# The inverse of chunks 4 to 7 kept in the other half of the partitions, in a fused two-layer decoder kernel

## The reference

```python
def step(state, inp):
    rt, wt, kt, vt, kkt, at = inp
    sa = jnp.einsum("bhvk,bhk->bhv", state, -kkt)
    state = (state * wt[:, :, None, :] + sa[..., None] * (kkt * at)[:, :, None, :]
             + vt[..., None] * kt[:, :, None, :])
    return state, jnp.einsum("bhvk,bhk->bhv", state, rt)
...
y = rwkv7_scan(r, decay, k, v, kk, a)
```

## Time and profile before

| what | value |
| --- | --- |
| median of 3 runs | 3664.91 us |
| profiled execution | 3667.72 us |
| its span | 3665.9 us |
| TensorE busy | 3335.7 us (91%) |
| VectorE busy | 1609.7 us (44%) |
| ScalarE busy | 1316.8 us (36%) |
| mean granted TensorE clock | 0.951 |

### The profile page before, as it was taken

The page is one execution under the profiler, slowest core; times in us unless marked ns, Lnnn a source line. Parts: engine busy times, 40 slices in busy tenths (PEclk is TensorE's granted clock), DMA queues, the critical chain, the costliest instruction groups (busy, mean ns, idle before and its releaser), DMA issues.

```text
span 3665.9 us, 76910 instructions
## 1 busy us (share of the span) xinstructions
PE 3335.7 (91%) x33546; PEld 2023.8 (55%) x33546; DVE 1609.7 (44%) x3443; ACT 1316.8 (36%) x2492; POOL 223.1 (6%) x345
## 2 busy tenths in 40 slices
PE   2898998899889858999999999999999999999998
PEld 1555465456446534666656466656556656556663
DVE  7254254335434534444554244454334454334442
ACT  0343243334333334333443233443324354323332
POOL 0010001010001000000000000000000000000000
PEclk8999999999999988999989999989999999999999
DMA  7231322223133121112011211111121111121111
GB/s 322 70 94 50 111 83 82 76 70 88 70 93 108 56 93 31 43 38 67 25 43 60 76 44 60 37 37 54 42 78 42 60 38 33 58 88 38 42 50 51
DMA packets 275847, 247.30 MB, mean 67 GB/s; under 512 B 16252, under 2 KB 251960, under 8 KB 272952
## 3 DMA queue, kind: packets, MB, share of 16 engines
q1 hardware_dynamic: 273208, 233.99, 20.2%
q0 software_dynamic: 2304, 8.39, 0.6%
HBM read 217.17 MB, written 25.18 MB: 66 GB/s over the span
## 4 chain that ended last, share of the span: by engine, by line
PE 76%; DVE 11%; DMA 5%; ACT 4%; issue 2%; SPq 1%; DVEq 0%; ACTq 0%; POOL 0%; another core or an unknown queue 0%
PE bank L655 20%; PE bank L529 14%; PE bank L624 6%; PE bank L739 4%; PE bank L752 4%; PE bank L562 3%; PE bank L748 3%; PE bank L526 3%; DVE xm L1534 3%; PE bank L604 3%; DVE arena L1595 2%; PE bank L666 2%; DMA xm<-in_ada_w 2%; PE bank L794 1%; DMA arena<-residual_scratch 1%
## 5 line engine op out<-in xcount | busy, mean ns | idle before, releaser
L655 PE MATMUL bank<-xm,wring 128*128 128x512 f32 x2048 | 947.8, 609 | 0.8 <-ACT arena L1083 0.8
L655 PEld LDWEIGHTS bank<-xm,wring 128*128 128x128 f32 x2048 | 386.5, 195 | 468.8 <-issue 457.6
L529 PE MATMUL bank<-arena,wring 128*128 128x512 f32 x1280 | 580.0, 593 | 13.4 <-ACT xm L948 5.1
L529 PEld LDWEIGHTS bank<-arena,wring 128*128 128x128 f32 x1280 | 231.0, 190 | 257.5 <-issue 246.0
L624 PE MATMUL bank<-wring,yT 128*128 128x512 f32 x776 | 346.6, 609 | 23.3 <-DVE yT L1427 10.1
L624 PEld LDWEIGHTS bank<-wring,yT 128*128 128x128 f32 x776 | 150.5, 195 | 216.4 <-issue 193.1
L1129 ACT COPY arena<-bank 128x256 f32<-128x256 f32 x256 | 96.4, 377 | 452.2 <-PE bank L752 452.2
L1802 POOL COPY r_Q<-ident 128x512 f32<-128x512 f32 x160 | 98.6, 616 | 2080.5 <-PE bank L752 2078.5
L1635 DVE COPY arena<-bank 128x64 f32<-128x64 f32 x256 | 57.5, 225 | 374.5 <-PE bank L784 369.6
L752 PE MATMUL bank<-arena,r_Q 64*64 64x32 f32 x5120 | 204.3, 223 | 0.0
L739 PE MATMUL bank<-arena 64*64 64x32 f32 x5120 | 196.4, 224 | 1.7 <-DVE arena L1619 1.0
(11 more groups left out here) (276 smaller groups left out, 5136.6 us busy)
## 6 DMA issues: line engine op xcount, KB each, us to landing
wring<-in_rw_w_rkvz SPq DMA_DIRECT2D x128, 512.0 KB, 4.4
wring<-in_ev_w_in SPq DMA_DIRECT2D x96, 512.0 KB, 5.3
xm<-in_ada_w SPq DMA_DIRECT2D x16, 1536.0 KB, 11.8
wring<-in_ev_w_out SPq DMA_DIRECT2D x32, 512.0 KB, 5.2
wring<-in_rw_w_out SPq DMA_DIRECT2D x32, 512.0 KB, 6.3
layer_input<-arena SPq DMA_DIRECT2D x4, 2052.0 KB, 7.6
wring<-layer_input SPq DMA_DIRECT2D x16, 513.0 KB, 6.8
xm<-in_x POOLq DMA_DIRECT2D x16, 512.0 KB, 5.4
```

The lines of the kernel that those rows point to most:

```text
L529: mm = pe.matmul(pj[:, :], w[:, k, :], hT[:, k, 1:1 + TB], start=(k == 0), stop=(k == KC - 1))
L655: mm = pe.matmul(bank[1 if m == PROJ_Z else 0][:, :], w[:, k, :], xmv[MIX_OF[m]][:, k, :], start=(k == 0), stop=(k == KC - 1))
```

## The change

The function tile gives for each chunk and head the half p (1 - h, where G and X are) and the half q, where Y and Q are; for chunks 0 to 3 q is p, for chunks 4 to 7 it is the other half. Start products of level 0 stay in p; from level 1 on they read p and write q. Columns products read q and write p, and transposed ones stay in q. Start products of all 8 chunks are one part now, and so are the columns products; in these parts chunk c and chunk c + 4 alternate. Transposed products stay in two parts. A level is start, transposed of group 0, transposed of group 1, columns. That makes 20 parts, and QUARTER_INV is new. The columns products wait for the transposed ones of their level. Y of chunks 4 to 7 is started by an extra product by the identity at level 1 and a predicated copy of its result, and no longer by VectorE's copies ahead of the first chunk. In chunks 4 to 7 the right-hand side and r_xs lie in the other half too, so that L771 and L784 stay in one half there, and L794 changes halves.

```diff
-QUARTER_INV = [[2, 1, 2, 1, 2, 0], [2, 1, 2, 1, 2, 0], [2, 1, 1, 1, 2, 0], [2, 1, 1, 1, 2, 0]]
+QUARTER_INV = [[1, 0, 1, 0, 2, 1], [1, 0, 2, 1, 0, 1], [2, 1, 0, 1, 0, 2], [1, 0, 1, 0, 1, 1]]
...
+    return (1 + (n - 1) // 4, (n - 1) % 4) if n else (0, 0)
...
+                def tile(c, h):
+                    return half_of(1 - h), half_of(h if c >= 4 else 1 - h), slice(c * 64, c * 64 + 64), c % 4 * 32
+
+                def start_of(c, h, k):
+                    p, q, cc, at = tile(c, h)
+                    return pe.matmul(packed(IV[c // 4][q if k else p, at:at + 32], 1 << k), G[p, gs_at(c, h):gs_at(c, h) + 64],
+                                     first(X[p, cc] if k else ident64[p, :], 1 << k), start=True, stop=True)
+
+                def columns(c, h, k):
+                    p, q, cc, at = tile(c, h)
+                    return pe.matmul(packed(IV[c // 4][p, 128 + at:160 + at], 1 << k), Y[q, cc], first(r_Q[q, k % 2, cc], 1 << k),
+                                     start=True, stop=True)
+
+                def transposes(c, h, k):
+                    p, q, cc, at = tile(c, h)
+                    return pe.matmul(packed(IV[c // 4][q, 256 + at:288 + at], 1 << k), r_Q[q, k % 2, cc], second(Y[q, cc], 1 << k),
+                                     start=True, stop=True)
...
+                        for c in range(4):
+                            for h in range(2):
+                                mm = start_of(c, h, k)
+                                if c == 3:
+                                    mm.then_inc(S["iq_ready"], 1)
+                            for h in range(2):
+                                mm = start_of(c + 4, h, k)
+                                if c == 3 and k != 1:
+                                    mm.then_inc(S["iqo_ready"], 1)
+                            if k == 1:
+                                for h in range(2):
+                                    p, q, cc, at = tile(c + 4, h)
+                                    mm = pe.matmul(IV[1][q, 256 + at:288 + at], ident64[p, :],
+                                                   second(G[p, gs_at(c + 4, h):gs_at(c + 4, h) + 64], 1), start=True, stop=True)
+                                    if c == 3:
+                                        mm.then_inc(S["iqo_ready"], 1)
...
+                        pe.wait_ge(S["iq"], v * 12 + 2 * k + g + 1)
                         if k == 1:
-                            pe.wait_ge(S["y0"], v + 1)
...
+                            for h in range(2):
+                                mm = transposes(c, h, k)
+                                if c == 4 * g + 3 and (g or k == LV_INV):
+                                    mm.then_inc(S["ixy_ready"], 1)
...
+                        for c in range(4):
+                            for h in range(2):
+                                mm = columns(c, h, k)
+                                if c == 3:
+                                    mm.then_inc(S["ixy_ready"], 1)
+                            for h in range(2):
+                                mm = columns(c + 4, h, k)
+                                if c == 3:
+                                    mm.then_inc(S["ixo_ready"], 1)
...
-                        pe.matmul(XB[half_of(1 - h), 0:64], G[r, g:g + 64], r_VT[r, c * RC:(c + 1) * RC], start=True, stop=False)
+                        pe.matmul(XB[at(c, h), 0:64], G[r, g:g + 64], r_VT[r, c * RC:(c + 1) * RC], start=True, stop=False)
...
+                    mm = pe.matmul(XB[at(c, h), 0:64], AR[r, c * P:c * P + 64], M[r, :], start=False, stop=True)
...
-                    mm = pe.matmul(XB[s, 64:128], Y[s, cc], r_xs[s, :], start=True, stop=True)
+                    mm = pe.matmul(XB[s, 64:128], Y[at(c, h), cc], r_xs[at(c, h), :], start=True, stop=True)
...
-                    y = Y[s, :].rearrange("p (a c x z) -> p a c x z", a=2, c=4, z=2)[:, :, :, :, 1]
-                    n = G[s, :].rearrange("p (a h c x z) -> p a h c x z", a=2, h=2, c=4, z=2)[:, :, h, :, 0:32, 1]
-                    for a in range(2):
-                        own(V.copy_predicated(y[:, a], umask[s, None, :].to_broadcast([64, 4, 32]), n[:, a]))
+                    y = Y[s, 0:256].rearrange("p (c x z) -> p c x z", c=4, z=2)[:, :, :, 1]
+                    n = G[s, :].rearrange("p (a h c x z) -> p a h c x z", a=2, h=2, c=4, z=2)[:, 0, h, :, 0:32, 1]
+                    own(V.copy_predicated(y, umask[s, None, :].to_broadcast([64, 4, 32]), n))
...
+                    V.wait_ge(S["iqo_ready"] if g else S["iq_ready"], 2 * (v * (LV_INV + 1) + k + 1))
...
+                    if k == 1 and g:
+                        V.copy_predicated(second(r_Y[v % 2][:, 256:512], 1).rearrange("p (c a) m -> p c (a m)", c=4),
+                                          umask[:, None, :].to_broadcast([P, 4, 32]),
+                                          IV[1][:, 256:384].rearrange("p (c x) -> p c x", c=4)).then_inc(S["y0"], 1)
```

More of the change, by code:

```diff
@@ L734, in invert @@
                         elif k == 1:
-                            pe.wait_ge(S["iq"], v * 12 + g + 1)
+                            pe.wait_ge(S["iq"], v * 12 + 2)
                         else:
-                            pe.wait_ge(S["ixy"], v * 10 + 2 * (k - 2) + g + 1)
-                        for c, h, r, cc, at in each:
-                            mm = pe.matmul(packed(IV[g][r, at:at + 32], m), G[r, gs_at(c, h):gs_at(c, h) + 64],
-                                           first(r_X[r, cc] if k else ident64[r, :], m), start=True, stop=True)
@@ L741, in invert @@
[L741 to L754 removed]
+                            pe.wait_ge(S["ixy"], v * 10 + 2 * (k - 2) + 2)
@@ L1629, in ahead @@
                     if v + 1 < NU:
[L1630 removed]
+                        rwkv_inverse(v + 1, COPY_CUT[3 * c + gap])
                 M = Mall[:, v % RP, :]
```

79 lines of the change are left out of this document (39 added, 40 removed).

## The result

The changed kernel takes 3679.69 us (median of 12 runs, 3675.74 to 3687.89) against 3668.8 for the kernel before timed beside it: ratio 1.0031, 95% interval 1.0022 to 1.0040, so slower by 8 to 15 us. The forecast of 3662 had the wrong sign: I had summed -3, the measurement says +11. That 3679.69 lies inside the stated range, 3637 to 3692, is owed to the width of that range and not to the sum.

A forecast was written before the change was run, and what follows sets the result against it. It took three TensorE-VectorE round trips per chunk, with floors of 0.66, 0.64 and 0.72 us, to bound the kernel. Units -4 and the first inverse +1 gave -3 us, so 3662 us, range 3637 to 3692.

The forecast's parts named there:

- Together -0.12 us per unit: Sum over an ordinary unit's four quarters, -0.18, -0.29, +0.72 and -0.37 us; over 31 units -4 us.
- my price: Inverse in each unit: an alternated part of 16 products costs 0.47 us, like a part of 8.
- The first inverse [...] +1: Inverse without chunks between its parts: waits for second copies 2.8 us, less 0.75 of (a) and some array time.
- (a): Unit start: VectorE makes two Y copies of 0.464 us instead of four; chunk 0's first gap -0.62 us.
- the fifth rival: Empty gaps pull the clock down, +11 us a unit, some +250 for most units; chance 0.02.
- Idle time over 0.2 us at the start of a level: Changed profile's inverse: TensorE idling this long there was listed as a sign that the forecast is wrong.
- (b) to (e): Units' inverse: slipping past blocked, columns 0.25 us behind transposed, levels await both 0.377 us ScalarE copies, late 0.326 us predicated copy.
- the second rival: Units' waits are shorter than reckoned; a unit 0.55 us shorter, -17 us, 3645; chance 0.21.
- The third: Rival: inner chain longer, four levels from 2 on 0.2 us late, +0.8 a unit, +25, 3687; chance 0.21.
- The four tiles: Alternated parts: four 64x64 tiles run at once, four instructions per slot of about 0.058 us.
- Array time: Inverse: 3.8 us less per unit, nearly all lost; the rival that it counts, -130 us, 3532, chance 0.03.
- at the same difference: Lower-clock stretches: same change as at full clock, despite parts counting double and TensorE waiting for VectorE's mixing at block changes.

The follow-up runs named there:

- the thin kernel: Changed kernel with each part of the inverse issuing only its last chunk's products, three quarters of the array work left out: 3534.78 us, 0.9650 of the kernel before.
- e4_mix: Changed kernel with the inverse ahead of the first unit spread among K steps of two projections: 3673.58 us, 1.0020 of the kernel before.
- e1_ycopies: Changed kernel with VectorE's two removed starting copies of Y put back: 3700.17 us, 1.0087 of the kernel before.
- the thin kernels: Kernel before and changed kernel, each with three quarters of the inverse's array work left out: 3544.5 us (0.9668) and 3534.78 us (0.9650).
- e1_serial: Changed kernel with alternation undone, chunks 0 to 3 of a double part ahead of chunks 4 to 7: 3735.05 us, 1.0180 of the kernel before.
- e2_tail: Changed kernel with QUARTER_INV's third row [2,1,0,1,2,0], moving two transposed parts out of the third quarter's last gap: 3682.92 us, 1.0041 of the kernel before.
- the thin kernel before: Kernel before with three quarters of the inverse's array work left out, every part, wait and copy kept: 3544.5 us, 0.9668 of the kernel before.

## Why the prediction was wrong

The two profiles of each kernel, from the first start product on, differ by 8.3 us in the mean:

```
first inverse (58.4, 58.4; after 62.6, 64.3)      +5.0
unit 0                                            -0.3
13 ordinary units                                 +1.5
15 units at block changes                         +2.0
unit 29, unit 30 (+1.9) and the last (-1.7)       +0.1
```

The ratios of the two timings say 9 and 11; the 1 to 3 us more I can't place. Against my sum of -3 two steps failed.

- **The step that failed for the most: "Together -0.12 us per unit".** An ordinary unit came out at +0.13 to +0.14. Over 31 units that is +4 for -4, some 8 us of the miss; the first inverse has 4. The quarters are 14.97, 12.81, 12.60 and 17.19 against my 14.86, 12.81, 12.53 and 17.11: the mechanism was right, and the sizes were off by a few hundredths in many gaps, in both directions, with no quarter shorter than forecast. Three terms make up most of it. First, chunk 0's first gap is 1.13 for 1.08, and for another reason than I gave: I let VectorE allow 0.95 and had level 0's array work set the gap, but the two copies take 0.93 us alone where the four had taken 1.49, and they set it. It is the same with three quarters of the array work gone. Second, an alternated part costs up to 0.05 more than my price where nothing covers it: chunk 1's last gap +0.57 for +0.52, chunk 4's second 0.98 for 0.93. Third, in chunks 5 and 6 the second gaps are 0.77 and 0.72 where I had 0.67 and 0.64. There L849's two pairs start 0.09 apart, with L852's between them; but in the thin kernel they start 0.10 apart and the gaps are 0.66, so that isn't the reason. It goes with the array work of the part ahead of L849 (in chunk 5 that part's predicated copy also starts so late that L1696 stands behind it); how it does so in chunk 6 stays open. The other way, chunk 3's last gap is 0.08 shorter than forecast and the first gaps of chunks 5 and 6 0.06.
- **The second step: "The first inverse [...] +1".** Measured: +4.2 and +5.9. What I left out is the lower clock. These stretches have 6.8 and 10.2 us more of it than before; at half their length that is 3.4 and 5.1 us, and without it both profiles say +0.8, near my +1. That nearness is partly luck, since two of its terms missed in opposite ways: the waits are 3.5 us (three of 0.76, three of 0.41) where I had 2.8, and (a) and the array time took off about as much more than I had. My sum has no term for the clock outside the units: I looked for that threat in the empty gaps alone, and those left it at 1.00, as the fifth rival's "against" had it. Idle time over 0.2 us at the start of a level was on my own list of signs of being wrong; it came here and not in the units. The kernel e4_mix has both waits and clock out of the way and its stretch is 57.3 us.
- **(a)** was right in direction, -0.57 for -0.62, confirmed by e1_ycopies from the other side. What limits the gap then was wrong, as said.
- **(b) to (e), the waits:** right in place, and in ordinary units about as large as I had them: chunk 4's second gap took even 0.05 more, chunk 5's first 0.06 less. So the second rival, which had them at nothing, falls by the table of gaps. The third falls by the thin kernels, which leave next to nothing of the waits. What it describes happens in the first inverse, where I hadn't put it.
- **The four tiles:** right; 32 instructions in 0.50 us, and e1_serial's 58 us is the price of not alternating them. What I had wrong is the price without alternation, 0.94 for 0.66 to 0.70.
- **Array time:** that nearly all of the 3.8 us would be lost was right, and why was half said. In both kernels TensorE's own products and about one part fit under a round trip. Eight empty gaps give that room away, and the four last gaps of the quarters, which cover nothing, took +0.57, +0.38, +0.70 and +0.31. These 1.96 us and the 0.34 in chunk 4's second gap are 2.30 of the 2.77 us by which gaps grew, against 2.65 by which the others shrank.
- **Block changes "at the same difference":** held in the sum (+2.0 us in 15 units), but units there scatter by more than that, so it isn't shown; and e2_tail shows that it needn't hold, since there a part moved away lets TensorE arrive early and wait for VectorE.

## What to carry to other kernels

Work that is hidden under round trips is worth only what stands out over them: before taking it away, add up by how much each gap exceeds its floor, not how busy the engine is. An order with fewer, longer dependent parts needs something to stand between them, and the place to look first is where it has no cover at all, such as the first pass before the pipeline fills. And a filling order tuned on the steady state must be read again at the places where another engine sets the pace or the clock is low.

## What the runs showed of the hardware

The clock can fall behind short waits. In the thin kernel before, chunk 0 of a unit has one wait of 1.18 us, and in every second ordinary unit the granted clock falls about the end of chunk 1's first gap and stays down into the projection, 6.8 us in all, though TensorE is busy there all the time. In the units between, with the same wait, it stays at 1.00, so the wait alone doesn't decide it. The wait, and by windows chunk 0 with that gap and the rest of the quarter, in a unit where it falls:

```profile
2240.65 0.33 PE L794 MATMUL bank<-arena,ident 64*64 64x64 f32 x4 [1.18 <-DVE arena L1635]
```
```profile
2238.96:2242.70 3.74, 2.53 (x72) 2.04 (x68) 3.44 (x12) 1.18 (x3) 0.00 (x0) 0.96 0.47 140
2242.70:2256.10 13.40, 13.39 (x58) 6.07 (x60) 3.02 (x5) 4.34 (x7) 0.62 (x1) 0.76 0.01 2
```

That unit takes 56.0 us instead of 53.2, and the kernel spends 253 us at the lower clock from unit 0's first chunk on against 184 and 187 in the two profiles of the kernel before: leaving work out gave 4.3 us a unit and took part of it back. Before, the same place idles for 0.48 us and the clock stays at 1.00.
